# Low parts of two half groups per chunk made by a negative copy on ScalarE and an accumulating transfer, in a two-layer decoder kernel

## The reference, cut to what matters

```python
def swiglu_ffn(x, norm_g, w_gate, w_up, w_down):
    h = rms_norm(x, norm_g)
    return (jax.nn.silu(h @ w_gate) * (h @ w_up)) @ w_down

def reference(x, ...):
    for layer in range(2):
        x = x + (chunked_sgu_mixer(...) if layer == 0 else moba_attention(...))
        x = x + swiglu_ffn(x, ffn_norm[layer], ffn_w_gate[layer], ffn_w_up[layer], ffn_w_down[layer])
    return x
```

## Time and profile before

| what | value |
|---|---|
| median of three runs | 2087.09 us |
| profiled execution, first to last instruction (span) | 2084.3 us |
| around the span (difference of the two) | 2.8 us |
| PE busy | 2078.5 us, 100% of the span |
| DVE busy | 1646.7 us, 79% |
| ACT busy | 1118.2 us, 54% |
| POOL busy | 42.2 us, 2% |
| DMA | 403.18 MB, mean 193 GB/s |
| PE's granted clock | 1.000 |

### The profile page before, as it was taken

How to read it: one execution, slowest core, us unless ns; L and a number is a source line. 1 busy time by engine, 2 the same in 40 slices (tenths; PEclk the granted TensorE clock), 3 DMA queues, 4 the chain that set the end, 5 groups by cost and what they waited for, 6 DMA issues and landing times.

```text
span 2084.3 us, 24255 instructions
## 1 busy us (share of the span) xinstructions
PE 2078.5 (100%) x9454; PEld 1725.8 (83%) x9454; DVE 1646.7 (79%) x1817; ACT 1118.2 (54%) x1362; POOL 42.2 (2%) x47
## 2 busy tenths in 40 slices
PE   9999999999999999999999999999999999999999
PEld 8888888888888888888888888888888888888887
DVE  5466579899889998988566666579899889988987
ACT  6444555555445554546666665465555455554553
POOL 1000000000000000000011001000000000000000
PEclk9999999999999999999999999999999999999999
DMA  9655546656565565555554454446556565566554
GB/s 328 205 176 180 179 147 233 209 182 205 199 219 175 199 214 196 189 182 202 192 185 168 148 192 164 162 161 232 192 191 213 185 219 182 202 210 202 178 188 150
DMA packets 203612, 403.18 MB, mean 193 GB/s; under 512 B 8080, under 2 KB 8688, under 8 KB 203248
## 3 DMA queue, kind: packets, MB, share of 16 engines
q1 hardware_dynamic: 202720, 398.50, 56.3%
q0 software_dynamic: 784, 3.19, 0.4%
HBM read 399.56 MB, written 2.10 MB: 193 GB/s over the span
## 4 chain that ended last, share of the span: by engine, by line
PE 98%; DVE 1%; ACT 0%; DMA 0%; SPq 0%; issue 0%
PE acc L1544 19%; PE acc L1542 19%; PE acc L1543 19%; PE acc L1401 10%; PE acc L1405 10%; PE acc L1403 10%; PE tr L1544 2%; PE tr L1543 2%; PE tr L1542 2%; PE tr L1449 2%; DMA raw<-in_a_w_in_dram 0%; PE tr L1706 0%; PE tr L1512 0%; PE tr L1680 0%; PE tr L1690 0%; PE tr L1698 0%
## 5 line engine op out<-in xcount | busy, mean ns | idle before, releaser
L686 ACT ACTIVATE w_hi<-raw 128x1024 fp32r<-128x1024 f32 x360 | 367.4, 1053 | 205.8 <-PE acc L1544 192.2
L1092 DVE TENSOR_TENSOR w_lo<-raw,w_hi 128x1024 fp32r<-128x1024 f32 x360 | 428.0, 1219 | 29.0 <-ACT w_hi L686 29.0
L1542 PE MATMUL acc<-w_hi,a_hi 128*128 128x512 f32 x896 | 350.2, 391 | 0.0
L1544 PE MATMUL acc<-w_hi,a_lo 128*128 128x512 f32 x896 | 348.8, 389 | 0.0
L1543 PE MATMUL acc<-w_lo,a_hi 128*128 128x512 f32 x896 | 348.6, 389 | 0.0
L1401 PE MATMUL acc<-w_hi,a_hi 128*128 128x512 f32 x640 | 254.7, 398 | 0.1
L1405 PE MATMUL acc<-w_hi,a_lo 128*128 128x512 f32 x640 | 249.7, 390 | 0.0
L1403 PE MATMUL acc<-w_lo,a_hi 128*128 128x512 f32 x640 | 249.2, 389 | 0.0
L676 ACT ACTIVATE s_hi<-sums_b 128x1024 fp32r<-128x1024 f32 x168 | 170.9, 1054 | 143.8 <-DVE sums_b L1087 130.8
L898 DVE TENSOR_TENSOR w_lo<-raw,w_hi 128x1024 fp32r<-128x1024 f32 x127 | 153.5, 1225 | 117.6 <-ACT w_hi L525 117.6
L676 ACT ACTIVATE s_hi<-raw 128x1536 fp32r<-128x1536 f32 x84 | 124.8, 1485 | 144.5 <-PE acc L1544 144.5
(11 more groups left out here) (217 smaller groups left out, 3438.4 us busy)
## 6 DMA issues: line engine op xcount, KB each, us to landing
raw<-in_ffn_w_down_dram SPq DMA_DIRECT2D x68, 1024.0 KB, 5.0
raw<-in_ffn_w_gate_dram SPq DMA_DIRECT2D x46, 1024.0 KB, 5.3
raw<-in_ffn_w_up_dram SPq DMA_DIRECT2D x46, 1024.0 KB, 5.1
raw<-in_ffn_w_gate_dram SPq DMA_DIRECT2D x84, 512.0 KB, 3.9
raw<-in_ffn_w_up_dram SPq DMA_DIRECT2D x84, 512.0 KB, 4.9
raw<-in_a_w_in_dram SPq DMA_DIRECT2D x30, 1024.0 KB, 5.3
raw<-in_ffn_w_down_dram SPq DMA_DIRECT2D x40, 512.0 KB, 5.0
raw<-in_a_w_out_dram SPq DMA_DIRECT2D x16, 1024.0 KB, 4.9
```

The lines of the kernel that those rows point to most:

```text
L686: nc.scalar.activation(w_hi[:, m % RING, :, :], raw[:, slot, half * HG:(half + 1) * HG, :], ACT.Copy)\
L1092: nc.vector.tensor_tensor(w_lo[:, m % RING, :, :], raw[:, slot, half * HG:(half + 1) * HG, :], w_hi[:, m % RING, :, :].bitcast(F32), ALU.s ...
L1542: nc.tensor.matmul(bank[:, :], hi, rhs_hi, start=start, stop=False)
L1544: return nc.tensor.matmul(bank[:, :], lo, rhs_hi, start=False, stop=stop)
```

## The change

In chunks 1 to 10 of both layers the half groups g5 and g6 (the table `ADDED`; 40 half groups in all) get their low part in another way. ACT, behind the high part, writes a second activation, the raw weights times -1, into `w_lo`; the output type rounds it, so that it is minus the high part. POOL waits for it (`neg_ready`) and issues a transfer that reads the same 512 KB of raw weights from HBM again and adds them to what is in `w_lo`; when it has landed (`lo_added`, one semaphore for each place of the ring), `w_lo` holds raw minus high. PE waits for `lo_added` in front of these half groups. DVE leaves out its subtraction for them. SP waits for the landing of g6's transfer before it reuses the slot of `g5 g6`. The counts of `lo_split` leave these half groups out (`n_split`), which shifts constants everywhere but moves nothing. On POOL, `head_norms` is defined earlier, all transfers of layer 0 are issued ahead of `norm(2)` and the mask, and those of layer 1 behind `norm(3)`.

```diff
--- before.py
+++ after.py
@@ -94,6 +94,10 @@
              "down 1": loads_of("g2 g3,g4 g5,g6 g7,s0,u2 u3,u4 u5,s1,u6 u7"),
              "down middle": loads_of("g2 g3,g4 g5,s0,u2 u3,s1,u4 u5")}
 
+
+
+    ADDED = {"chunk": items("g5 g6"), "first": [], "down 0": [], "down 1": [], "down middle": []}
+
     def kind(k):
 
         if k[1] == "chunk":
@@ -113,6 +117,7 @@
 
     HG_OF, PAIR_OF, LOAD_OF, BOTH_OF, LAST_PAIR, END_OF, DOWN_HG, NUMBER = {}, {}, {}, {}, {}, {}, {}, {}
     PAIRS_BEFORE, DOWN_LOAD = {}, {}
+    ADDED_HG = []
 
     FORMS = {}
 
@@ -146,6 +151,8 @@
                         n_pair += 1
                     else:
                         HG_OF[k, item] = hg
+                        if item in ADDED[kind(k)]:
+                            ADDED_HG.append(hg)
                         hg += 1
                 LAST_PAIR[k], END_OF[k] = n_pair - 1, hg
                 for load in loads(k):
@@ -155,6 +162,7 @@
                         LOAD_OF[k, item], BOTH_OF[k, item] = len(reads) - RAW, n_both[slot]
                     end = load[-1]
                     reads.append(("pair", PAIR_OF[k, end[1]] + 1) if end[0] == "s" else
+                                 ("added", HG_OF[k, end]) if end in ADDED[kind(k)] else
                                  ("half group", HG_OF[k, end] + 1))
         assert hg % RING == 0 and len(reads) % RAW == 0
         if layer == 0:
@@ -163,6 +171,20 @@
             hg = hg_before["wo"] + NC * KB // HG
     HG_END = hg
     LAYER_LOADS = len(SLOT_READ[0]) - RAW
+
+    def n_split(n):
+
+        return n - sum(1 for m in ADDED_HG if m < n)
+
+    def n_neg(m):
+
+        return ADDED_HG.index(m) + 1
+
+    def n_added(m):
+
+        return sum(1 for n in ADDED_HG if n <= m and n % RING == m % RING)
+
+    qkv_split = hg_before["qkv"] - n_split(hg_before["qkv"])
 
     def in_slot(load):
 
@@ -287,6 +309,7 @@
         raw_landed = [sem(f"raw_landed{s}") for s in range(RAW)]
         hi_split = sem("hi_split")
         lo_split = sem("lo_split")
+        neg_ready, lo_added = sem("neg_ready"), [sem(f"lo_added{n}") for n in range(RING)]
         w_used = sem("w_used")
         staged = sem("staged")
         transposed = sem("transposed")
@@ -367,7 +390,12 @@
             def slot_free(layer, n):
 
                 what, count = SLOT_READ[layer][n - RAW]
-                sp.wait_ge(s_split if what == "pair" else lo_split, count)
+                if what == "pair":
+                    sp.wait_ge(s_split, count)
+                elif what == "added":
+                    sp.wait_ge(lo_added[count % RING], 16 * n_added(count))
+                else:
+                    sp.wait_ge(lo_split, n_split(count))
 
             def block_loads(k, w_first, w_second, n):
 
@@ -420,7 +448,7 @@
                     n = down(layer, p, n)
 
             feed_forward(0)
-            base = hg_before["qkv"]
+            base = hg_before["qkv"] - qkv_split
             load_unit(w_v_k, 0, base)
             load_unit(w_k_k, 0, base + 8)
             load_unit(w_q_k, 0, base + 16)
@@ -429,8 +457,8 @@
                 load_unit(w_k_k, i * CH, i * 24 + (base + 8))
                 load_unit(w_q_k, i * CH, i * 24 + (base + 16))
             for n, (c, g) in enumerate(WO_FIRST):
-                load(n % RAW, w_o_k[:, 4 * g:4 * g + 4, c * CH:(c + 1) * CH], hg_before["wo"] + 2 * n - 6)
-            load_unit(w_o_k, (NC - 1) * CH, (NC - 1) * 8 + hg_before["wo"])
+                load(n % RAW, w_o_k[:, 4 * g:4 * g + 4, c * CH:(c + 1) * CH], hg_before["wo"] - qkv_split + 2 * n - 6)
+            load_unit(w_o_k, (NC - 1) * CH, (NC - 1) * 8 + hg_before["wo"] - qkv_split)
             feed_forward(1)
             for c in range(NC - 1):
 
@@ -480,6 +508,27 @@
             pool.wait_ge(mv_ready, 1)
             inverse_root(ln_rstd[:, :], ln_mv[:, :, 1], 1.0, EPS, ln_rstd_ready)
             norm(1)
+
+            def head_norms(i):
+                for n, (scale, eps) in enumerate(((1.0 / P, EPS), (1.0, EPS * P))):
+
+                    pool.wait_ge(kq_ss, i * 2 + (n + 1))
+                    src = head_ss[:, n, :, :].rearrange("p t h -> p (t h)")
+                    dst = head_rs[:, n, :, :].rearrange("p t h -> p (t h)")
+                    inverse_root(dst, src, scale, eps, kq_rs)
+
+            def add_raw(layer):
+                for k in (k for k in NUMBER if k[0] == layer):
+                    for item in order(k):
+                        if item not in ADDED[kind(k)]:
+                            continue
+                        m = HG_OF[k, item]
+                        pool.wait_ge(neg_ready, n_neg(m))
+                        w = (w_gate_k if item[0] == "g" else w_up_k)[layer]
+                        src = w[:, HG * item[1]:HG * item[1] + HG, k[2] * CH:(k[2] + 1) * CH]
+                        pool.dma_start(w_lo[:, m % RING, :, :], src, accum_op=ALU.add).then_inc(lo_added[m % RING], 16)
+
+            add_raw(0)
             norm(2)
             step.inc(nc.gpsimd.memset(mask[:, :, :], 0.0))
             step.wait()
@@ -487,18 +536,10 @@
 
                 nc.gpsimd.affine_select(out=mask[:, n, :], in_=mask[:, n, :], compare_op=ALU.is_ge, fill=NEG,
                                         base=0, pattern=[[-1, P]], channel_multiplier=1).then_inc(mask_ready, 1)
-
-            def head_norms(i):
-                for n, (scale, eps) in enumerate(((1.0 / P, EPS), (1.0, EPS * P))):
-
-                    pool.wait_ge(kq_ss, i * 2 + (n + 1))
-                    src = head_ss[:, n, :, :].rearrange("p t h -> p (t h)")
-                    dst = head_rs[:, n, :, :].rearrange("p t h -> p (t h)")
-                    inverse_root(dst, src, scale, eps, kq_rs)
-
             for i in range(NC):
                 head_norms(i)
             norm(3)
+            add_raw(1)
 
 
         @block.scalar
@@ -683,8 +724,10 @@
             def plain_hi(m, slot, half, sem_landed, count):
                 act.wait_ge(sem_landed, 16 * count)
                 act.wait_ge(w_used, m - (RING - 1))
-                nc.scalar.activation(w_hi[:, m % RING, :, :], raw[:, slot, half * HG:(half + 1) * HG, :], ACT.Copy)\
-                    .then_inc(hi_split, 1)
+                src = raw[:, slot, half * HG:(half + 1) * HG, :]
+                nc.scalar.activation(w_hi[:, m % RING, :, :], src, ACT.Copy).then_inc(hi_split, 1)
+                if m in ADDED_HG:
+                    nc.scalar.activation(w_lo[:, m % RING, :, :], src, ACT.Copy, scale=-1.0).then_inc(neg_ready, 1)
 
             def forms_hi_part(n, dst):
 
@@ -1183,7 +1226,7 @@
                         slot, _ = in_slot(LOAD_OF[k, item])
                         if item[0] == "s":
                             pair_lo(PAIR_OF[k, item[1]], slot)
-                        else:
+                        elif item not in ADDED[kind(k)]:
                             load, = [w for w in loads(k) if item in w]
                             plain_lo(HG_OF[k, item], slot, load.index(item))
                         for work in hooks.get(item, ()):
@@ -1390,7 +1433,7 @@
 
                 first = isinstance(m, int) and m == 0
                 if not first:
-                    pe.wait_ge(lo_split, m + 1)
+                    pe.wait_ge(lo_split, n_split(m + 1) if isinstance(m, int) else m + 1)
                 for k in range(HG):
                     kb = HG * j + k
                     if first:
@@ -1409,7 +1452,7 @@
             def last_pair(m, s, j, j0):
 
 
-                pe.wait_ge(lo_split, m + 2)
+                pe.wait_ge(lo_split, n_split(m + 2))
                 for t in range(TT):
                     tok = slice(t * P, (t + 1) * P)
                     for d in range(2):
@@ -1545,7 +1588,10 @@
 
             def plain_group(m, lhs_hi, lhs_lo, q, s, start, stop):
 
-                pe.wait_ge(lo_split, m + 1)
+                if m in ADDED_HG:
+                    pe.wait_ge(lo_added[m % RING], 16 * n_added(m))
+                else:
+                    pe.wait_ge(lo_split, n_split(m + 1))
                 for k in range(HG):
                     kb = HG * q + k
                     for t in range(TT):
```

## The result

The changed kernel takes 2096.33 us (median of four runs, 2094.79 to 2097.81); the kernel before takes 2087.09. The ratio is 1.0044 with a 95% interval of 1.0032 to 1.0057: slower by 9.2 us, a quarter of the 35 us that were forecast. The profiled execution took 2096.11 us, 1.7 us more than its span of 2094.4 us; the span grew by 10.1. (The 2.8 us that I put around the span of the kernel before were too much: in the 27 executions timed beside the first experiments 2.1 to 2.2 us lie around it. The difference of the medians is 9.2 all the same.)

What follows compares the result with a forecast made beforehand. PE was taken to bound the kernel, its matmuls filling 2078.5 of 2084.3 us. Waits for the new transfers, 20 x 7.8 - 121.1 = 34.9 us, plus 2084.3 and 2.8 around it gave 2122 us; range 2086 to 2178.

Steps and rivals of the forecast that it cites:

- What bounds the kernel, and where the loss would lie: PE busy 2078.5 of 2084.3 us; freeing DVE gives nothing; new waits only at the first matmuls of g5 and g6.
- The leads: Time from the negative copy's end to PE's use: 6.69, 6.26, 5.90, 4.95 us; 121.1 us over 20 chunks.
- L: Time from POOL's issue of the 512 KB accumulating transfer to its landing: 7.7 us, between 6.2 and 8.2.
- a load through SP: Plain 512 KB load on SP's queue, from issue to landing: 3.9 us, the base for the new transfer.
- the software queue: Extra time for issuing the transfer through POOL instead of SP: 2.3 us, with 2.8 as the upper bound.
- the second read: The accumulating transfer reads two sources per byte written: 1.5 us more, with bounds of nothing and 1.5.
- rival 1: Transfer lands in time, at most about 6.0 us after issue: no change, 2087 us (2085 to 2091); chance 0.17.
- The hops: The two semaphore hops around the transfer, before POOL's issue and after the landing: 0.1 us together.
- The sum: PE's wait at g5 and g6: 20 x 7.8 - 121.1 = 34.9 us, everything else costed at nothing.
- Rival 2: Addition in the transfer much slower than two reads: 65 to 147 us of waits, 2152 to 2234 us; chance 0.23.
- Rival 3: Raw slot for the u3 u4 load comes late, landing after 434.83; at 11 us, 2150 us; chance 0.03.
- The clock: PE's granted clock, at full level in every slice; no row shows a wait's effect, so no change taken.

## Why the prediction was wrong

**What bounds the kernel, and where the loss would lie: right.** In the chunks PE waits at the first matmul of g5 and g6 and nowhere else; freeing DVE brought nothing; `u3 u4` was never late.

**The leads: right to 0.15 us.** Worked out as 6.69, 6.26, 5.90 and 4.95 us. They can be read where no transfer is late, in the kernel without the addition, from the end of each copy to PE's matmul: 6.69, 6.38 to 6.42, 5.89 and 4.95 to 4.99. Only the second was off, 0.14 us too short in the mean, in 14 chunks 2.0 us in all. The experiments built on these leads came within 2 us.

**L, the time from issue to landing: the step that failed.** It was 3.9 (a load through SP) + 2.3 (the software queue) + 1.5 (the second read) = 7.7 us. It measured 6.1. The first term is right and the third nearly (2.2, of which 1.3 are the packets and 0.5 POOL's longer issue). The second is the one that failed: without the addition the landing is 3.9 us, which leaves nothing of it beside the first term, and counted at the first packet, as I had counted it, it is 0.5 us (1.42 against 0.9). I had read 2.3 us from a transfer that waited 3.2 us for its first packet. In rows 12 the other queue filled 92.6% of the engines. The experiments with the early load show what that does: 2.3 us more to the first packet of a plain transfer. What I took for a property of the queue was, by these numbers, the price of company (the transfer of rows 11 itself was not repeated without it), and in the chunks there is none, since SP waits for this very landing. I had noted the idle queues under rival 1 and did not let them into the sum.

**The hops: too small.** Taken as 0.1 us, they are 0.30 from the copy to POOL's issue and 0.04 from the landing to PE. With L = 6.1 and 0.34: 20 x 6.44 - 121.1 = 7.7 us, and 5.7 with the leads as measured, which add up to 123.1. Of the 8.8 us measured, 6.7 lie at the first matmuls. The 1.0 between is the scatter of L, from 5.9 to 6.6 us: a late landing costs and an early one gives nothing back, and with each landing's own time against its own lead the sum is 7.0. The other 2.1 us lie at the second matmuls, a term that the sum did not have: behind 18 of these waits the second start is 0.34 us behind the first in place of 0.23.

**The sum** multiplies an error of L by 20, so 1.4 us too much in L and hops together were 27 us too much in the total; with L near the lead, a price that was off by a fifth gave a result off by a factor of four. The range of 2086 to 2178 us held the time, since it reached to the case of a landing within the lead.

**Rival 1** (in time, no change) was nearer in size than the forecast. The Trainium skill's formula for a software transfer (DMA: Bandwidth & Descriptors, Anatomy of one DMA) gives 3.2 us as an estimate where 3.9 was measured without the addition. **Rival 2** did not happen. **Rival 3** was right that the slot matters, with the roles turned round: the landing that holds the load back is what keeps the queues empty for the transfer. It is the earlier release that costs 105 us. **The clock** did not fall in the changed kernel, whose waits are 1.3 us at most; in the experiments it fell behind 22 of the 23 waits of over 2.5 us, and twice behind shorter ones, of 1.96 and 2.49.

No kernel here is faster than before. Nothing that DVE gives up is on PE's path, so the best version, with the copy first, is level with it. Using DVE's free time for a fourth pair in each chunk was not tried.

## What to carry to other kernels

When work is moved off an engine that nobody waits for, the best that can come out is no change; ask only whether the new path fits in the lead, and measure the lead from the trace for each kind of place, since the shortest ones pay. Take the price of a transfer from a stretch with the same neighbours in the queues: the same 512 KB landed after 6.1 us alone and after 9.9 beside a load. A wait that looks too careful (the slot released only at the landing) can be what keeps a queue clear, so measure what it does before taking it away. And where lead is short, put the instruction that starts the long chain first.

## What was not expected of the hardware

- A plain software transfer of 512 KB that moves alone lands after 3.9 us, the median of SP's loads of this size, which have another beside them; POOL's issue takes 0.72 us of that, with the addition 1.20, and for the two halves of the bytes 0.85 and 1.20.
- An accumulating transfer's packets of 2 KB last 178 ns against 99 without the addition, so the engines bring little more than half the rate.
- A load of 1 MB through SP, issued from 0.27 us ahead to 0.7 us behind a software transfer, puts off its first packet by 1.8 to 2.9 us (medians of three experiments); issued 4.1 us behind, it does not matter.
- After a wait of 4.1 us TensorE ran at the lower clock level for some 3.4 us. It did so once after a wait of 1.96 us and once after 2.49, and not after one of 2.41.
